# Two first feed-forward slices of a hybrid decoder step: half-size products in alternating order

## The reference

```python
hn = rms_norm(h, norm_ffn_g)
return h + (jax.nn.silu(hn @ w_gate) * (hn @ w_up)) @ w_down     # 1024 -> 2816 -> 1024
```

## Time and profile before

| what | value |
|---|---|
| time, median of 3 runs | 1287.11 us (1286.85 to 1287.22) |
| the profiled execution's own time | 1287.07 us |
| its span, first to last instruction | 1285.3 us |
| mean granted TensorE clock | 0.995 of full speed |
| TensorE busy | 1262.8 us, 98% of the span |
| VectorE, ScalarE, GpSimd busy | 516.0, 378.0, 646.0 us |

### The profile page before, as it was taken

One profiled execution on the slowest core, in us unless ns is written; L12 is line 12 of the kernel. 1 busy time (PEld: TensorE's weight loads), 2 busy tenths in 40 slices (PEclk: granted clock), 3 DMA queues, 4 the chain that ended last, 5 costly groups with the idle time before them and its releaser, 6 DMA issues.

```text
span 1285.3 us, 21876 instructions
## 1 busy us (share of the span) xinstructions
PE 1262.8 (98%) x9082; PEld 1174.3 (91%) x9082; DVE 516.0 (40%) x942; ACT 378.0 (29%) x715; POOL 646.0 (50%) x529
## 2 busy tenths in 40 slices
PE   7999999999999999998999999999999999999997
PEld 7997788989666699998999999999999999999997
DVE  7844213433766432677323232323232323232146
ACT  6000110100677611354332323232323232323323
POOL 3453023323455341047756666666666666656735
PEclk9999999999999999998999999999999999999999
DMA  5546366252111051011112021212120212121203
GB/s 202 194 148 222 111 240 241 97 213 83 50 67 67 1 188 48 2 34 34 66 34 66 34 66 34 66 34 67 34 67 34 66 34 66 36 65 36 80 1 136
DMA packets 38098, 107.99 MB, mean 84 GB/s; under 512 B 4016, under 2 KB 16496, under 8 KB 36208
## 3 DMA queue, kind: packets, MB, share of 16 engines
q1 hardware_dynamic: 38000, 106.60, 24.1%
HBM read 95.73 MB, written 10.85 MB: 83 GB/s over the span
## 4 chain that ended last, share of the span: by engine, by line
PE 92%; DVE 3%; ACT 2%; issue 1%; POOL 1%; DMA 0%; DVEq 0%; SPq 0%; ACTq 0%
PE ps L1154 11%; PE ps L1156 11%; PE ps L1155 11%; PE ps L1188 7%; PE ps L1190 7%; PE ps L1189 6%; PE ps L719 6%; PE ps L721 6%; PE ps L720 6%; PE ps L859 3%; PE ps L904 3%; PE ps L883 2%; PE ps L928 2%; PE ps L929 2%; PE ps L930 2%; PE ps L836 1%
## 5 line engine op out<-in xcount | busy, mean ns | idle before, releaser
L1154 PE MATMUL ps<-combo,w_hi 128*128 128x264 f32 x672 | 192.7, 287 | 3.5 <-issue 3.5
L1156 PE MATMUL ps<-combo,w_lo 128*128 128x264 f32 x672 | 192.0, 286 | 0.0
L1155 PE MATMUL ps<-combo,w_hi 128*128 128x264 f32 x672 | 191.8, 285 | 0.0
L588 POOL TENSOR_TENSOR w_lo<-w_stage,w_hi 128x512 fp32r<-128x512 f32 (+1 forms) x57 | 77.5, 1361 | 183.3 <-ACT w_hi L1213 183.2
L1980 DVE TENSOR_TENSOR resid<-ps,resid 128x352 f32<-128x352 f32 x240 | 126.0, 525 | 103.5 <-PE ps L1190 103.5
L719 PE MATMUL ps<-act_hi,w_hi 128*128 128x352 f32 x480 | 158.9, 331 | 7.9 <-DVE act_lo L1642 7.9
L1188 PE MATMUL ps<-hid,w_hi 128*128 128x352 f32 x504 | 163.1, 324 | 0.7 <-DVE resid L1980 0.7
L1190 PE MATMUL ps<-hid,w_lo 128*128 128x352 f32 x504 | 162.5, 322 | 0.0
L1189 PE MATMUL ps<-hid,w_hi 128*128 128x352 f32 x504 | 162.3, 322 | 0.0
L721 PE MATMUL ps<-act_hi,w_lo 128*128 128x352 f32 x480 | 155.2, 323 | 0.0
L720 PE MATMUL ps<-act_lo,w_hi 128*128 128x352 f32 x480 | 155.0, 323 | 0.0
(11 more groups left out here) (328 smaller groups left out, 3002.0 us busy)
## 6 DMA issues: line engine op xcount, KB each, us to landing
w_stage<-in_w SPq DMA_DIRECT2D x75, 512.0 KB, 3.6
resid<-in_state_k SPq DMA_DIRECT2D x8, 1792.0 KB, 7.8
v_buf<-in_state_v SPq DMA_DIRECT2D x14, 1024.0 KB, 5.0
raw<-in_w SPq DMA_DIRECT2D x22, 512.0 KB, 3.5
resid<-in_xT SPq DMA_DIRECT2D x16, 528.0 KB, 7.7
out_yT<-resid SPq DMA_DIRECT2D x24, 176.0 KB, 1.8
q_d<-out SPq DMA_DIRECT2D x12, 176.0 KB, 4.1
out_kT<-out SPq DMA_DIRECT2D x12, 176.0 KB, 1.9
```

The lines of the kernel that those rows point to most:

```text
L588: pool.tensor_tensor(w_lo_row[:, cols_], half_unit(f, product), f32(w_hi_row[:, cols_]), ALU.subtract).then_inc(half_split, 1)
L1154: pe.matmul(out, hi[:, wk], x_hi[:, k, tk], start=(k == 0 and first), stop=False, skip_group_check=not first)
L1155: pe.matmul(out, hi[:, wk], x_lo[:, k, tk], start=False, stop=False, skip_group_check=not first)
L1156: mm = pe.matmul(out, lo[:, wk], x_hi[:, k, tk], start=False, stop=(k == 3), skip_group_check=not first)
```

## The change

TensorE's order from U2 on becomes (1,P7), (2,P1), (1,P4), (1,P6), (2,P2), (1,P5), (2,P7), (2,P6), (1,P3), (2,P5), (2,P4), (2,P3). GpSimd's and ScalarE's lists follow it, with the hidden instructions of slices 0 and 1 at other places between; `weight_high(1, "P7")` and `weight_high(2, "P1")` stand ahead of S3's copies, S4's copies ahead of slice 0's hidden copies. `keep_p7(1)` no longer waits for `hidden2`. VectorE runs `plain_hidden` ahead of S2's remainders and the s4 combinations behind S1's remainders. The places of these products in the ring are given by a table, `FIRST_POS`.

```diff
@@ gpsimd, -644
             weight_low(1, "P2")
             last_weight_sum(1)
             weight_low(1, "P7")
+            weight_low(2, "P1")
+            weight_low(1, "P4")
             weight_low(1, "P6")
-            weight_low(1, "P4")
+            weight_low(2, "P2")
             weight_low(1, "P5")
-            weight_low(2, "P1")
+            weight_sums(2)
+            weight_low(2, "P7")
+            hidden_low2(0)
+            weight_low(2, "P6")
+            hidden_low1(0)
+            last_weight_sum(2)
             weight_low(1, "P3")
-            hidden_low2(0)
-            hidden_low1(0)
-            weight_sums(2)
-            weight_low(2, "P2")
-            last_weight_sum(2)
-            weight_low(2, "P6")
             second_hidden(1)
+            weight_low(2, "P5")
             hidden_low2(1)
-            weight_low(2, "P7")
-            weight_low(2, "P5")
-            hidden_low1(1)
             weight_low(2, "P4")
             weight_low(2, "P3")
+            hidden_low1(1)
@@ scalar, -1360
             def keep_p7(f):
                 act.wait_ge(gate_done, GATE_NO[f, "P7"])
-                act.wait_ge(hidden2, f)
+                if f > 1:
+                    act.wait_ge(hidden2, f)
                 copy(b3, two_banks(0)).then_inc(p7_kept, 1)
@@ scalar, -1458
                 combo_high(A22, y22, k, Y22_AT[k])
+            weight_high(1, "P7")
             keep_p1(1)
+            weight_high(2, "P1")
             for k in range(4):
                 combo_high(S3, s3_f, k, S3_AT[k])
             silu_second(0)
-            weight_high(1, "P7")
+            weight_high(1, "P4")
             weight_high(1, "P6")
             for k in range(4):
                 combo_high(S2, y11, k, S2_AT[k])
-            weight_high(1, "P4")
+            weight_high(2, "P2")
             weight_high(1, "P5")
-            weight_high(2, "P1")
-            weight_high(1, "P3")
             act.wait_ge(gate_done, GATE_NO[0, "U2"])
-            for k in range(4):
+            for k in range(2):
                 combo_high(S1, y21, k, S1_AT[k])
             keep_p7(1)
-            hidden_high2(0)
-            keep_u2(1)
-            hidden_high1(0)
+            for k in range(2, 4):
+                combo_high(S1, y21, k, S1_AT[k])
+            silu_first(1)
             act.wait_ge(dve_lo, 20)
             for k in range(4):
                 combo_high(S4, y12, k, S4_AT[k])
-            weight_high(2, "P2")
-            silu_first(1)
+            weight_high(2, "P7")
+            hidden_high2(0)
+            hidden_high1(0)
+            keep_u2(1)
             weight_high(2, "P6")
+            keep_p1(2)
             silu_second(1)
-            keep_p1(2)
+            weight_high(1, "P3")
+            weight_high(2, "P5")
             hidden_high2(1)
-            weight_high(2, "P7")
-            weight_high(2, "P5")
-            hidden_high1(1)
             weight_high(2, "P4")
             weight_high(2, "P3")
+            hidden_high1(1)
@@ vector, -2039
             combined(y11, y21, y11, 3, ALU.subtract, S1_AT[3])
+            plain_hidden()
             for k in range(4):
                 combo_low(20, y11, S2, k)
             for k in range(4):
+                combo_low(24, y21, S1, k)
+            for k in range(4):
                 combined(y12, y12, y11, k, ALU.subtract, S2_AT[k])
-            plain_hidden()
-            for k in range(4):
-                combo_low(24, y21, S1, k)
             for k in range(4):
                 combo_low(28, y12, S4, k)
             second_gate(1)
@@ tables, -2147
-FIRST_GATES = [(0, "G1"), (0, "U1"), (1, "P1"), (1, "P2"), (0, "G2"), (0, "U2"), (1, "P7"), (1, "P6"), (1, "P4"), (1, "P5"),
-               (2, "P1"), (1, "P3")] + [(2, n) for n in PRODUCTS[1:]]
+FIRST_GATES = [(0, "G1"), (0, "U1"), (1, "P1"), (1, "P2"), (0, "G2"), (0, "U2"), (1, "P7"), (2, "P1"), (1, "P4"), (1, "P6"),
+               (2, "P2"), (1, "P5"), (2, "P7"), (2, "P6"), (1, "P3"), (2, "P5"), (2, "P4"), (2, "P3")]
+FIRST_POS = {(0, "G"): 0, (0, "U"): 2, (1, "P1"): 4, (1, "P2"): 5, (1, "P7"): 10, (2, "P1"): 11, (1, "P4"): 6, (1, "P6"): 7,
+             (2, "P2"): 8, (1, "P5"): 9, (2, "P7"): 12, (2, "P6"): 13, (1, "P3"): 14, (2, "P5"): 15, (2, "P4"): 16, (2, "P3"): 17}
@@ lay_out, -2191
         else:
-            POS[what], GATE_AT[pos] = pos, GATE_NO[what]
+            POS[what] = FIRST_POS.get(what, pos)
+            GATE_AT[POS[what]] = GATE_NO[what]
```

More of the change, by code:

```diff
@@ L2190, in lay_out @@
             if what[1][1] == "1":
-                POS[0, what[1][0]] = pos
+                POS[0, what[1][0]] = at = FIRST_POS[0, what[1][0]]
                 SPLIT_NO[0, what[1][0]] = splits = splits + 1
-                GATE_AT[pos] = GATE_AT[pos + 1] = GATE_NO[0, what[1][0] + "2"]
+                GATE_AT[at] = GATE_AT[at + 1] = GATE_NO[0, what[1][0] + "2"]
                 pos += 2
         else:
-            POS[what], GATE_AT[pos] = pos, GATE_NO[what]
+            POS[what] = FIRST_POS.get(what, pos)
+            GATE_AT[POS[what]] = GATE_NO[what]
             SPLIT_NO[what] = splits = splits + 1
```

## The result

The changed kernel takes 1292.03 us (median of 6 runs, 1291.48 to 1292.79) against 1287.12 (6 runs, 1286.85 to 1287.35): **4.9 us slower**, ratio 1.0038 [1.0026, 1.0051]. Its profiled execution took 1291.48 us, with a span of 1289.7 against 1285.3.

What follows compares the result with a forecast made beforehand. TensorE was taken as the bound, busy 98% of the span, with 10.8 us lost in the edited stage. Terms 0.9 + 6.6 + 2.4 + 2.8 + 1.7 = 14.4 give 3.6 us slower, 1290.7; range 1285.5 to 1293.2.

Steps and rivals of the forecast that it cites:

- The sum, 14.4 lost: Expected total loss in the twelve products from (1,P7) to (2,P3), in place of 10.8 us before.
- What goes: The losses of 0.4 us before (1,P4) and 3.6 us in (1,P4) would go.
- (2,P1), +0.9: (2,P1) would wait 0.9 us for plain_hidden, where before it waited for nothing.
- The wait ahead of (1,P5), +6.6: TensorE would wait 6.6 us for keep_u2(1) ahead of (1,P5), with VectorE and GpSimd alternating; 3.55 before.
- the third rival: GpSimd shut out by VectorE and the clock late: upper terms, 16.8 us lost, 1293.1 us; chance 0.13.
- my upper bound of 604.6: Latest start of (1,P5), with GpSimd shut out until S4's last remainder at 594.3: a wait of 7.6 us.
- The clock behind it, +2.4: The lower clock level after the wait ahead of (1,P5) would cost 2.4 us; bounds 1.7 and 3.4.
- (2,P5), +2.8: (2,P5) would start 2.8 us later behind (1,P3), waiting for keep_u2(2) on ScalarE; bounds 2.4 and 3.2.
- The clock behind that, +1.7: The lower clock after the wait ahead of (2,P5) would cost 1.7 us; bounds 0 and 1.7.
- At no cost: The later first down weight load, list and ring order and silu_second(0) would cost nothing; down weights stay covered.
- The first rival: The port costs nothing here: (1,P5) waits 0.3 us, 4.8 lost against 10.8, 1281.1 us; chance 0.12.
- one of the signs I had named as proof that I was wrong: The forecast is wrong if VectorE keeps 0.62 us through GpSimd's work.

Runs made afterwards that it cites:

- e6_p7only: The kernel before, with only keep_p7(1)'s wait for hidden2 taken out: 1287.42 us, ratio 1.0.
- e1_break: The changed kernel with a one-column memset on VectorE behind the third S2 remainder: 1289.72 us, ratio 1.002.
- e7_selfwait: The changed kernel, in which VectorE's fourth S2 remainder first waits for the third to have ended, with no added instruction: 1290.18 us.
- e3_p5: The changed kernel with first_gate(2) ahead of first_hidden(1) on VectorE, silu_first(2) and keep_u2(2) ahead of hidden_high1(1) on ScalarE: 1288.46 us.
- e2_lists: The changed kernel with hidden_low2(0) ahead of weight_sums(2) on GpSimd, slice 0's hidden copies and keep_u2(1) ahead of weight_high(2,P7) on ScalarE: 1287.17 us.
- e8_sums: The changed kernel with e2_lists' and e3_p5's edits, weight_sums(2) on VectorE, a memset behind S1's third remainder, weight_high(2,P7) ahead of keep_u2(1): 1282.71 us.
- e9_gate: e8_sums with VectorE's four S4 remainders behind second_gate(1) in place of ahead of it: 1280.46 us.

## Why the prediction was right, and where it was not

The forecast was 3.6 us slower, 1290.7; it is 4.9 slower, 1292.03, inside the range. The sum, 14.4 lost, comes near the 14.9 of the trace, but two of its terms were off, by +2.0 and -1.7 us, and it is luck that they nearly made up for each other.

- **What goes.** Right: no wait and no lower clock in (1,P4) and (1,P6), 5.82 us for two products. `e6_p7only`, with one part of the edit alone, gains nothing.
- **(2,P1), +0.9.** It lost 1.05, behind `plain_hidden` as said.
- **The wait ahead of (1,P5), +6.6: the step that failed.** "I take 6.6, since the rows nearest in kind, S1's remainders at 588.84, alternate." They did not alternate. GpSimd was shut out from 586.06 to the end of VectorE's run, the mechanism of the third rival, which had 0.13. Two things follow. (2,P2) itself waited 1.94 us for its remainder and was followed by 3.41 us at 1.2 GHz, 3.75 us that the sum doesn't have: I had spoken of (2,P2) only with first_gate(1). And (1,P5) started at 605.86, not 603.6, behind my upper bound of 604.6 too: that let GpSimd in at 594.3, but the run ended at 595.30, and by my own 592.6 and four remainders of 0.62 it should have been 595.1. In place of 6.6 the two stretches hold 3.75 + 4.84 = 8.6. `e1_break` and `e7_selfwait` show that the missing gap in VectorE's run is the cause: with one, GpSimd's row falls to 2.35 us, (2,P2) has no wait, and (1,P5) starts at 603.8 after 6.5 us of waiting, the forecast's term.
- **Where I chose wrongly.** The alternating remainders of before each came behind a break in VectorE's run: S1's behind plain_hidden, which reads PSUM, S4's behind a wait of 3.90 us. The 4.79 us row stood in the middle of a run, and it ended only behind `plain_hidden`, which broke that run at 588.22. The change puts `plain_hidden` ahead of the remainders, so that sixteen instructions follow without that break, and the 4.79 us row was the nearer one. The product at 577.05, which got in between s1 and s2 combinations, is the exception; no run tells why. The Trainium skill, SBUF — State Buffer, section Who interferes with whom, gives the shared ports to whoever starts first, for its whole instruction. By that GpSimd would have waited for one instruction of 0.62 us; fifteen or so ended while its row stood at 10.36. Where the two alternate the trace agrees with that page; in this unbroken run it doesn't.
- **The clock behind it, +2.4.** (1,P5) took 5.27 us from its first matmul to its end at 611.13, 2.36 more than undisturbed. Right.
- **(2,P5), +2.8.** 2.84, by the chain named; `e3_p5` removes it.
- **The clock behind that, +1.7.** It didn't come: 8.83 us for three products at a clock of 1.00, where my lower bound of 0 held. In `e2_lists` it did come behind the same wait, so a wait of that length doesn't settle it; what does stays open. Without this term the sum gives 1.9 us slower, and `e1_break`, in which the two engines alternate as the prediction had it and the clock doesn't fall here either, is 2.2 slower.
- **At no cost.** TensorE's waits from 632 us on are 0.9 us in sum before and after, so nothing in the down projection waited for what was costed at nothing; the later down weights were covered.

The first rival, that the port costs nothing, falls with `e1_break`: contested pairs took 1.7 us. The Trainium skill, Advanced Engine Details and Errata, section VectorE Performance Modes, names only two-port instructions as those that GpSimd's interfere with. By that these differences would run free of GpSimd; the trace is against it here. (The times that doubled are those of the earlier trace rows; GpSimd's product in the earlier trace rows grew by a third, from 1.3 to 1.75.) What VectorE kept (0.62 through GpSimd's work, one of the signs I had named as proof that I was wrong) was paid by GpSimd alone, and cost more.

## What to carry to other kernels

Before work is put together on VectorE, look whether GpSimd has float32 products in the same stretch: an unbroken run of VectorE instructions with two SBUF operands can keep one of them waiting until the run ends (10.36 us here), so a pause belongs ahead of what TensorE needs first. A pause only decides whose turn it is; the later start that needed both engines' work, (2,P7), moved here only when one of them had less of it and what isn't urgent (the S4 remainders) stood behind what is. And a wait that is removed pays only down to the next one under it: here the gain at (1,P4) was void as long as (1,P5) came no earlier.

## What the hardware showed that I had not expected

- A GpSimd product of 1.28 us stood for 10.36 us beside sixteen back-to-back VectorE differences at 0.62 us each, which lost nothing; a memset of 0.06 us, or one wait for the instruction ahead, brought it down to 2.35.
- Two GpSimd products, at 577.05 before and at 596.12 in `e8_sums`, got in at the end of one VectorE instruction (1.55 and 1.82 us) with no pause that the trace shows.
- Once GpSimd is in, the two alternate for as long as it has work queued: 1.7 us a pair in `e1_break`, five products long; then VectorE's run closes again (2.32 us for the product asked for at 599.38, until the last instruction of the run).
- The granted clock fell behind the 2.68 us wait ahead of (2,P5) in `e2_lists` (0.50 from 618.31 to 621.73) and not in the kernel after, and behind the 1.94 us wait ahead of (2,P2) in the kernel after (0.50 from 597.27) and not behind the same wait, 1.95 us, in `e3_p5`. In `e9_gate`, with no wait over 1.5 us in this stage, it stayed at 1.00.
